# Self-attention scores and part of its value products in f32r parts, in a one-core decoder layer

## What is computed

```python
def one_block(args):
    q_blk, i = args
    sc = jnp.einsum('bqhd,bkhd->bhqk', q_blk, k).astype(jnp.float32) * scale
    q_pos = i * ATTN_BLOCK + jnp.arange(ATTN_BLOCK)
    mask = key_pos[None, :] <= q_pos[:, None]
    p = jax.nn.softmax(jnp.where(mask, sc, -jnp.inf), axis=-1).astype(v.dtype)
    return jnp.einsum('bhqk,bkhd->bqhd', p, v)
...
mix = jnp.concatenate([ret, sgu, mla], axis=-1) @ w_out
x = layer_norm(DEEPNORM_ALPHA * x + mix, ln_mix_g[l], ln_mix_b[l])
```

## Time and profile before

| | |
|---|---|
| median of 3 runs | 1046.35 us (1041.05 to 1046.6) |
| the profiled execution | 1040.7 us, span 1038.8 us |
| PE busy | 983.9 us, 95% of the span |
| DVE, ACT, POOL busy | 608.5, 353.7, 193.9 us |
| mean granted TensorE clock | 0.988 of full speed |
| attend, first matmul to last DVE instruction | 269.4 to 438.6 us |

### The profile page before, as it was taken

How to read it: one execution, slowest core, us unless ns; L and a number is a source line. 1 busy time by engine, 2 the same in 40 slices (tenths; PEclk the granted TensorE clock), 3 DMA queues, 4 the chain that set the end, 5 groups by cost and what they waited for, 6 DMA issues and landing times. The chain is left out here.

```text
span 1038.8 us, 15837 instructions
## 1 busy us (share of the span) xinstructions
PE 983.9 (95%) x5619; PEld 827.2 (80%) x5619; DVE 608.5 (59%) x1276; ACT 353.7 (34%) x737; POOL 193.9 (19%) x273
## 2 busy tenths in 40 slices
PE   7999999999899999899998999999999999999994
PEld 5898877676778887778886788887888989888883
DVE  6644341677566665455553544648666676767575
ACT  5122031434344343331010434232144444545341
POOL 0012100111000000002220000000634544343534
PEclk9999999999799999999999999999999999999998
DMA  8022010000599000091013200003788888889872
GB/s 333 15 82 81 1 62 1 1 1 2 219 414 413 16 1 1 16 349 41 21 61 124 81 1 2 1 24 139 310 258 294 257 298 303 309 303 328 288 258 86
DMA packets 63736, 150.47 MB, mean 145 GB/s; under 512 B 10304, under 2 KB 12608, under 8 KB 63680
## 3 DMA queue, kind: packets, MB, share of 16 engines
q1 hardware_dynamic: 54720, 132.77, 36.2%
q0 software_dynamic: 8960, 16.96, 4.4%
HBM read 109.46 MB, written 54.92 MB: 158 GB/s over the span
## 5 line engine op out<-in xcount | busy, mean ns | idle before, releaser
L1672 PEld LDWEIGHTS h_ps<-xgT,e_gate_up 128*128 128x128 f32 x1024 | 153.9, 190 | 4.5 <-DVEq L1762 2.2
L1672 PE MATMUL h_ps<-xgT,e_gate_up 128*128 128x176 f32 x1024 | 155.5, 313 | 2.1 <-DVEq L1762 2.1
L245 PE MATMUL unit_ps<-whi,xhi 128*128 128x512 f32 (+1 forms) x256 | 98.6, 385 | 9.6 <-DVE wlo L276 9.6
L246 PE MATMUL unit_ps<-wlo,xhi 128*128 128x512 f32 (+1 forms) x256 | 98.3, 384 | 0.0
L247 PE MATMUL unit_ps<-whi,xlo 128*128 128x512 f32 (+1 forms) x256 | 98.0, 383 | 0.0
L725 PEld LDWEIGHTS o_ps<-mla_v,prob_T 128*128 128x128 f32 x576 | 71.9, 196 | 15.8 <-issue 11.1
L704 PE MATMUL s_ps<-mla_kT,mla_qT 96*128 96x512 f32 (+3 forms) x192 | 73.2, 509 | 3.6 <-PEq L2023 3.6
L725 PE MATMUL o_ps<-mla_v,prob_T 128*128 128x64 f32 x576 | 72.1, 276 | 2.6 <-ACT prob_T L760 2.4
L245 PEld LDWEIGHTS unit_ps<-whi,xhi 128*128 128x128 f32 x256 | 48.7, 190 | 18.1 <-DVE xlo L315 7.4
L1790 DVE SCALAR_TENSOR_TENSOR z<-y_ps,slot_weight,x_rows 128x512 f32<-128x512 f32 (+1 forms) x64 | 45.7, 746 | 17.9 <-PE y_ps L1686 12.7
L1736 ACT ACTIVATE ln_junk<-z,z_neg_mean 128x1024 f32<-128x1024 f32 (+1 forms) x32 | 36.8, 1149 | 56.6 <-DVE z_neg_mean L1795 56.1
(11 more groups left out here) (297 smaller groups left out, 1960.4 us busy)
## 6 DMA issues: line engine op xcount, KB each, us to landing
e_gate_up<-w_gu SPq DMA_DIRECT2D x16, 2048.0 KB, 10.3
e_down_raw<-w_dn SPq DMA_DIRECT2D x16, 1024.0 KB, 5.2
slot_rows<-zeros SPq DMA_DIRECT2D x22, 522.0 KB, 14.9
slot_sums<-zeros SPq DMA_DIRECT2D x22, 512.0 KB, 15.3
x_rows<-slot_rows SPq DMA_DIRECT2D x16, 522.0 KB, 4.6
slot_sums<-z SPq DMA_DIRECT2D x16, 512.0 KB, 4.1
wraw<-w_in SPq DMA_DIRECT2D x24, 256.0 KB, 4.7
xraw<-xT SPq DMA_DIRECT2D x8, 512.0 KB, 6.9
```

What stands on the lines that cost most here:

```text
L245: pe.matmul(o, hi, whi[:, s, 0:w], start=(s == 0), stop=False)
L246: pe.matmul(o, hi, wlo[:, s, 0:w], start=False, stop=False)
L1672: end = pe.matmul(hps[:, m, gu * CAP:(gu + 1) * CAP], gate_up[:, b, s, w], xT[:, s, :], start=(s == 0), stop=(s == KD - 1))
```

## The change

1. **Scores from tile 3 on** (`SPLIT = 3`) are three f32r products, q_hi k_hi, q_hi k_lo and q_lo k_hi. The high parts are made by ACT, the low parts by POOL, tile by tile during attend; `k_lo` and `q_lo` are written over `kT` and `qT`. `qT` is laid out by token tile now.
2. **Values of part 0 from tile 4 on** (`V_SPLIT = 4`): ACT rounds the turned probabilities to `probT_hi`, and DVE then writes the rest to `probT_lo`, from PSUM. For each of the first four key tiles PE multiplies `probT_hi` with high and low values side by side (128 columns) and `probT_lo` with the high values (64 columns). `take` works in halves of four heads and from tile 4 on adds the two column groups first. On ACT the copies of unit u-1 stand ahead of the exponential of unit u there.
3. `probT_lo` lies where `zeros` lies, so its first use waits for all 44 transfers of zeros.
4. **Queue of SP**: the zeros go first; a slice of `w_out` is loaded over the queries of a finished tile, after the zeros. In mix_out `g` and `b` are loaded after the split of the weights.
5. **Between prepare and attend**: the semaphore clear is now two instructions on POOL and no second barrier follows. The last tile's state update is left out (it isn't used), its normalisation and gating are done by DVE inside attend, at its third iteration, and DVE makes one half of the last `qT` copy.

The diff, cut to its core:

```diff
@@ prepare
-                for j in range(2):
-                    act.activation(k.qT[0:MQ, 4 * j:4 * j + 4, tok],
+                for j in range(2 if t + 1 < NT else 1):
+                    act.activation(k.qT[0:MQ, t, 4 * j:4 * j + 4, :],
...
+                if t + 1 < NT:
...
+                else:
+                    dve.wait_ge(q_t, NT)
+                    dve.tensor_scalar(k.qT[0:MQ, t, 4:8, :], ps[0:MQ, 4, :].rearrange("p (h t) -> p h t", t=P), MLA_SCALE, None, ALU.mult)\
+                       .then_inc(qT_copied, 1)
@@ attend
+    probT_hi = at("prob_T_hi", 20, [P, 2, 4 * P], f32r)
+    probT_lo = at("prob_T_lo", 185, [P, 2, 4 * P], f32r)
     zeros = at("zeros", 185, [P, ROW])
...
+    nc.clear_and_free_semaphores([s for s in k.used[:older] if s is not k.ret_rstd_ready])
...
-            for s in range(KD):
-                sp.dma_start(k.w_out_raw[:, s, :], A["w_out"][s * P:(s + 1) * P, :]).then_inc(k.w_out_loaded, 16)
             sp.wait_ge(zeroed, 1)
...
+            for s in range(KD):
+                sp.wait_ge(scored, units.index((s + 1, 0)) if s + 1 < NT else len(units))
+                sp.dma_start(k.w_out_raw[:, s, :], A["w_out"][s * P:(s + 1) * P, :]).then_inc(k.w_out_loaded, 16)
@@ scores(u)
+                        pe.matmul(out, q_hi[0:MQ, i % 2, h, :], k_hi[0:MQ, h, keys], start=True, stop=False)
+                        pe.matmul(out, q_hi[0:MQ, i % 2, h, :], k_lo[0:MQ, h, keys], start=False, stop=False)
+                        last = pe.matmul(out, q_lo[0:MQ, i, h, :], k_hi[0:MQ, h, keys], start=False, stop=True)
@@ values(u)
+                        if u >= FIRST and j == 0:
+                            pe.matmul(ops[:, h // 4, c:c + 2 * MV], probT_hi[:, u % 2, p], v_parts[:, m, h, :], start=(m == 0), stop=False)
+                            last = pe.matmul(ops[:, h // 4, c:c + MV], probT_lo[:, u % 2, p], v_parts[:, m, h, 0:MV], start=False, stop=False)
@@ scalar
+            def turned_high(v):
+                act.wait_ge(p_t, 2 * v + 1)
+                act.wait_ge(pv_done, v - 1)
+                act.activation(probT_hi[:, v % 2, :], tps[:, 0, :], ACT.Copy).then_inc(pT_hi_made, 1)
...
+                if u > FIRST:
+                    turned_high(u - 1)
+                    turned_copy(u - 1)
@@ vector
+                        if v == FIRST:
+                            dve.wait_ge(k.rows_zeroed, 16 * 2 * (SLOTS // P))
+                        dve.wait_ge(pT_hi_made, v - FIRST + 1)
+                        dve.tensor_tensor(probT_lo[:, v % 2, :], tps[:, 0, :], probT_hi[:, v % 2, :].bitcast(f32), ALU.subtract).then_inc(pT_copied, 1)
@@ mix_out
+            sp.wait_ge(w_lo, KD)
             sp.dma_start(g[:], over(A["ln_mix_g"], [P, D])).then_inc(loaded, 16)
             sp.dma_start(b[:], over(A["ln_mix_b"], [P, D])).then_inc(loaded, 16)
-
-            sp.wait_ge(w_lo, KD)
@@ program
-        if i == 1:
-
-            nc.clear_and_free_semaphores(used)
-            nc.all_engine_barrier()
```

More of the change, by code:

```diff
@@ L447, in prepare @@
             nc.Block() as block:
+        k.ret_last = on, mv4, rs4, ps
         @block.tensor
@@ L510, in _ @@
                 last.then_inc(out_sum, 1)
-                pe.wait_ge(kd_made, t + 1)
-                for j in range(2):
[L514 to L517, removed]
-                if t + 1 < NT:
+                if t + 1 < NT:
+                    pe.wait_ge(kd_made, t + 1)
+                    for j in range(2):
+                        last = pe.matmul(ps[:, 6, j * P:(j + 1) * P],
+                                         kd[:, b, 2 * j:2 * j + 2, :].rearrange("p h d -> p (h d)"),
+                                         k.rv[:, t, j * P:(j + 1) * P], start=True, stop=True)
+                    last.then_inc(kv_sum, 1)
                     latents_T(t + 1)
@@ L611, in _ @@
                                              sgb[:, g:g + 1], k.su[:, t, g * SD:(g + 1) * SD], ALU.add, ALU.mult)
[L613 to L618, removed]
@@ L658, in attend @@
     at, A, cst = k.at, k.dram, k.cst
+    SPLIT, V_SPLIT = 3, 4
     prob = at("prob", 12, [P, 2, 2, 4 * P])
-    probT = at("prob_T", 20, [P, 2, 2, 4 * P])
+    probT = [at(f"prob_T{j}", 20 + 4 * j, [P, 2, 4 * P]) for j in range(2)]
+    probT_hi = at("prob_T_hi", 20, [P, 2, 4 * P], f32r)
+    probT_lo = at("prob_T_lo", 185, [P, 2, 4 * P], f32r)
+    v_parts = at("v_parts", 189.25, [P, V_SPLIT, MH, 2 * MV], f32r)
+    low_part = at("o_low_part", 205.25, [P, 4, MV])
     nmx = at("neg_max", 28, [P, 2, 2])
@@ L712, in turn @@
                         pe.wait_ge(pT_copied if j == 0 else pT_copied_act, u)
+                    if j == 0 and u > FIRST:
+                        pe.wait_ge(pT_hi_made, u - FIRST)
                     for m in range(z - a):
@@ L802, in _, with keys_low @@
+                    for i in range(NT):
+                        if v == units.index((i, 4)) + 1:
+                            take(i, 0)
+                        if i and v == units.index((i, 0)) + 1:
+                            take(i - 1, 1)
+            take(NT - 1, 1)
         @block.gpsimd
         def _(pool):
-            pool.memset(zeros[:], 0.0).then_inc(zeroed, 1)
+            def keys_low(t):
+                pool.wait_ge(k_hi_made, t + 1)
+                tok = slice(t * P, (t + 1) * P)
+                pool.tensor_tensor(k_lo[0:MQ, :, tok], k.kT[0:MQ, :, tok], k_hi[0:MQ, :, tok].bitcast(f32), ALU.subtract)\
+                    .then_inc(k_lo_made, 1)
@@ new lines, in queries_low @@
+            def queries_low(t):
+                pool.wait_ge(q_hi_made, t - SPLIT + 1)
+                pool.tensor_tensor(q_lo[0:MQ, t], k.qT[0:MQ, t], q_hi[0:MQ, t % 2].bitcast(f32), ALU.subtract)\
+                    .then_inc(q_lo_made, 1)
+            pool.memset(zeros[:], 0.0).then_inc(zeroed, 1)
+            pool.wait_ge(k_hi_made, SPLIT)
+            for h in range(0, MH, 2):
+                pool.wait_ge(scored, units.index((SPLIT - 1, h)) + 1)
+                heads, tok = slice(h, h + 2), slice(0, SPLIT * P)
+                pool.tensor_tensor(k_lo[0:MQ, heads, tok], k.kT[0:MQ, heads, tok], k_hi[0:MQ, heads, tok].bitcast(f32), ALU.subtract)\
+                    .then_inc(k_old_lo_made, 1)
+                if h == 0:
+                    keys_low(SPLIT)
+                if h == 2:
+                    queries_low(SPLIT)
@@ L812, in mix_out @@
+            for t in range(SPLIT + 1, NT):
+                keys_low(t)
+                queries_low(t)
+                if t == SPLIT + 1:
+                    for m in range(V_SPLIT):
+                        pool.wait_ge(v_hi_made, m + 1)
+                        pool.tensor_tensor(v_parts[:, m, :, MV:2 * MV], k.v[:, m, :].rearrange("p (h d) -> p h d", d=MV),
+                                           v_parts[:, m, :, 0:MV].bitcast(f32), ALU.subtract).then_inc(v_lo_made, 1)
 def mix_out(nc, k):
```

157 lines of the change are left out of this document (117 added, 40 removed).

## The result

The changed kernel takes **1076.97 us** (median of 1071.62, 1076.45, 1077.48 and 1096.16) against 1046.44 for the kernel before on the same chip: 2.8% slower, ratio 1.0281, 95% interval 1.0247 to 1.0316. The forecast was 1056.5 in a range of 1045 to 1070. The direction was right, the size was 30.5 us in place of 11.8, and the time lies above the range. The profiled execution took 1077.48 us, its span 1075.6.

A forecast was written before the change was run, and what follows sets the result against it. PE, busy 95% of the span, was taken to bound the kernel. Zeros landing 332.1 + 116.4 + clock 1.4 put attend's end at 449.9 (+11.3); with mix_out +11.8 on the mean 1044.7: 1056.5 us, range 1045 to 1070.

The forecast's parts named there:

- Part 1, PE's own sum: Attend: PE's work falls 8.6 us over 32 units of tiles 4 to 7, 1.4 in tile 3; narrow records 0.107 each.
- the load rows: Trace rows of PE weight loads, cited against quick narrow records: f32r's lasts 191 ns, f32's 196, bf16's 96.
- Both rivals on narrow records: Attend's narrow f32r records quicker (-10 us, chance 0.15) or dear (about +13 us, 1070, chance 0.15).
- Part 2, the chain: Tiles 4 to 7: two-step copy in series makes units 3.2, 3.4, 3.6, 3.95; first subtraction to attend's end 116.4 us.
- What f32r saves on PE is given back: Tiles 4 to 7: PE's savings return as waits for the copies, +0.8 us in all.
- POOL makes the low parts ... covered: Attend: 1024 columns take POOL at most 2.9 us, two of these per tile in over 25 us, so hidden.
- Part 3, the wait: Tile 4's first subtraction waits for zeros landing at 332.1, or 328 without the tail; PE held some 7 to 13 us.
- Part 3, the clock: Behind tile 4's wait PE's clock falls to half for 3.5 to 7 us, costing 1.4 to 2.8; 1.4 taken.
- the no-hold case: Rival: the zeros don't hold PE in tile 4, so only the other terms count; 1043 to 1045 us, chance 0.12.
- Part 4, mix_out: Mix_out: gains issued only after the weights' split land at 456.0, at most 457; +0.5 us (0 to 1.5).
- dear records: Rival in attend: each narrow f32r column costs four times a wide product's; about +13, 1070 us, chance 0.15.

The follow-up runs named there:

- e3: Changed kernel with f32r scores alone: values' products in f32 throughout, no wait for the zeros; 1028.88 us, ratio 0.9842.
- e5: e1 with a take that scales both parts in PSUM and adds them last; 1045.29 us, ratio 1.0005.
- e1: Changed kernel with the low part of the turned probabilities in its own memory, so no wait for the zeros; 1055.86 us, ratio 1.0097.
- e9: Changed kernel, wait for the zeros included, with the take of e5; 1072.08 us, ratio 1.0284.
- e2: Kernel before the change plus a wait for the zeros at tile 4's first copy; 1062.14 us, ratio 1.0165.
- e15: e9 with 14 products that nobody reads added on TensorE in the wait; 1065.86 us, ratio 1.0206.
- e13: Changed kernel with f32 scores and values throughout, plus a wait for the zeros at tile 4's first copy; 1054.9 us.
- e11: Changed kernel with f32 scores, f32r values, the wait for the zeros kept and the take of e5; 1063.2 us.
- e14: The kernel of e7 run again, beside e13 on the same chip; 1050.0 us.
- e7: e3 plus a wait for the zeros at the first copy of tile 4; 1048.4 us.
- e10: e9 with 28 products that nobody reads added on TensorE in the wait; 1063.35 us, ratio 1.0164.

## Why the prediction was wrong in size

- **Part 1, PE's own sum: right.** Narrow f32r value records are 0.11 us apart, the middle units of e3 are within 0.06 of the sums. The Trainium skill, page "TensorE: Matmul & The Clock Gate", section "Weight-path perf modes — Fast Weight Load (FWL) and DoubleRow", has the fast load on where there are 128 weights and the type is not FP32; if f32r were such a type, the records would have been quicker. The pace of 0.11 speaks against it, as the load rows did. Both rivals on narrow records fall.
- **Part 2, the chain: right in kind, 2 us short.** In e5, where the clock is up, the units take 3.28, 3.51, 3.73 and 4.00 for 3.2, 3.4, 3.6 and 3.95, and from the first subtraction to the end of attend it is 118.5 us for 116.4. The sentence "What f32r saves on PE is given back" is the main finding on the change itself: without the value part, 16 us are kept. The given-back time is idle time of TensorE, as forecast: pieces of 0.35 to 0.42 us a unit in tile 4 of e5, and one of 1.07 in tile 7.
- **"POOL makes the low parts ... covered": wrong reason.** They are in time (2.4 us for 1024 columns), but two of them block VectorE's take. Ahead of the change no step of `take` read two operands from SBUF. Where the wait is absent this costs 10.6 us (e1 to e5), up to 6 of them through the clock by the runs' half clock (55 us against 43).
- **Part 3, the wait: right.** Forecast 7 to 13 us on TensorE and a landing at 328 or 332; measured 9.41 and 328.5.
- **Part 3, the clock: this is the term that failed.** "After such a gap the clock falls ... 3.5 us lose 1.4, 7 us 2.8. I take 1.4." Measured: 51.2 us at half, in 46.5 of which TensorE was at work. I took the length from the two falls of the earlier trace rows, as if it were a property of the gap, and of the two I took the shorter and called the longer "at least 7 us". The trace before has that one in full, at the start of this same loop, behind 3.6 us of idle:

```profile
269.60:283.20 13.60, 12.58 (x52) 11.11 (x52) 6.76 (x17) 5.01 (x25) 0.69 (x1) 0.50 0.95 343
```

It is 13.6 us long with TensorE at work in 12.6; it would have given a term of 4 to 6 us, more than the 1.4 and still too little. In e9 against e5 the wait costs 26.8 us; my sum for it, 1056.5 less the 1044 of the no-hold case, was 12.5. That is 14 of the 18.7 us by which the sum fell short. Another 1 to 2 are that the no-hold kernel, e5, came out at +0.05% and not 1 us faster (the chain's 2.1 us, mix_out, and 17 us at half at the end of attend for 3.4). The last 3 us are within what the runs resolve. The split hangs on the order: from e1, with its collisions, to the changed kernel the wait brings only 20 us, because e1 has already lost 10; the two losses don't add.
- **Part 4, mix_out: a little low.** `ln_b` is waited for 1.45 us longer, forecast 0.5 with an end at 1.5.
- **The no-hold case: one slip.** Its own terms, -2.7 - 1.4 + 3.1 + 0.5 and 0 to -2 for the clock on the mean of 1044.7, give 1042 to 1044, not 1043 to 1045; e5 has 1045.3.
- **The range** bounded the price of records and the landing, and left the clock's cost between 1.4 and 2.8. Its top, 1070, came from dear records. With 24 us at half as a bound for the clock, as e2 later showed, the top would have lain some 10 us higher.

## What to carry to other kernels

Where an engine is busy without a break, price a new wait on it with what it does to the clock: here 12 us of idle cost 27, and 1.7 us of idle brought 37 us at half clock, where 1.5 us elsewhere brought none. A split that leaves the bounding engine's sum as it is but puts two engines' steps in series ahead of it only loses; take the part that lowers the sum (the scores) and leave the other. When a step moves onto POOL, look which of VectorE's steps beside it read two operands from SBUF.

## What the runs showed of the hardware

- A busy TensorE can stay at half clock: 28.00 of 28.00 us busy at 0.50 in the changed kernel, 32.00 of 32.00 in e15. The stretches behind the wait for the zeros ran from 10 to 51 us in the profiles; the part of them with TensorE at work was 5.8 and 10.8 us in the f32 kernels (e13, e2) and 22 to 47 us in those with f32r products (e11, e14, e9, e7, the changed one).
- Single idle stretches of 1.07 (e5, the end of tile 7), 1.51, 1.66 and 1.77 us (e1, e15) were each followed by half clock. Others were not: 1.04 and 1.52 us in the changed kernel, and the first of 1.07 us in e9, e10 and e15 (451.0, 445.5 and 450.0). Pieces of 0.42 us, 3.2 us in 28, weren't either (e5).
- VectorE's step with two SBUF operands took 2.09 us for 0.42 beside a POOL subtraction; with one of them in PSUM 0.42 to 0.43.
- An f32 product of 384 columns is two records of 0.32 us.
